# Router products from x1 itself, with the norm moved to weights and logits, and two embedding tiles and the slots' table moved back in TensorE's order

## What is computed

```python
x = x + mix                                    # conv and retention heads, out-projection
x = x + hier_moe(rmsnorm(x, norm2_g), ...)     # 4 groups of 8 experts
ple = rmsnorm(p @ w_ple, ple_norm_g)           # per-layer embedding
x = x + ple * jax.nn.sigmoid(x @ w_ple_gate)

def hier_moe(t, rg_w, rg_b, re_w, re_b, w_gate, w_up, w_down):
    g_prob = softmax(t @ rg_w + rg_b)          # one group
    e_logit = (t @ re_w + re_b)[that group]    # two experts of its eight
    hid = silu(t @ w_gate[e]) * (t @ w_up[e])
    y = (hid * combine) @ w_down[e]
```

## Time and profile before

| what | us |
|---|---|
| median of 3 runs | 692.66 |
| lowest and highest of them | 689.54 and 694.28 |
| the profiled execution, by the clock that timed the runs | 692.57 |
| its span in the trace | 690.8 |
| PE busy in the span | 658.1 |
| DVE, ACT, POOL busy | 575.2, 408.5, 248.6 |

### The profile page before, as it was taken

The page is one execution under the profiler, slowest core; times in us unless marked ns, Lnnn a source line. Parts: engine busy times, 40 slices in busy tenths (PEclk is TensorE's granted clock), DMA queues, the critical chain, the costliest instruction groups (busy, mean ns, idle before and its releaser), DMA issues.

```text
span 690.8 us, 11414 instructions
## 1 busy us (share of the span) xinstructions
PE 658.1 (95%) x3970; PEld 567.8 (82%) x3970; DVE 575.2 (83%) x808; ACT 408.5 (59%) x521; POOL 248.6 (36%) x182
## 2 busy tenths in 40 slices
PE   8999999998999999997999999999999999998996
PEld 5999999998998889846878888888878777766885
DVE  5599999987776474476899999999999999968785
ACT  7331322236262132375699999999999889862322
POOL 1151498979429230004233333333334343310001
PEclk9999999999999999997999999999999999999999
DMA  9651331121039272627489999999999999775211
GB/s 291 201 153 32 129 117 62 62 86 49 1 99 317 77 243 101 234 110 248 173 353 381 374 374 378 367 378 394 394 390 377 379 377 371 292 290 188 77 61 62
DMA packets 49532, 156.10 MB, mean 226 GB/s; under 512 B 6938, under 2 KB 28634, under 8 KB 36427
## 3 DMA queue, kind: packets, MB, share of 16 engines
q1 hardware_dynamic: 35905, 133.98, 51.6%
q10 hardware_dynamic: 9346, 12.13, 5.3%
q0 software_dynamic: 4240, 9.44, 3.8%
HBM read 143.55 MB, written 17.59 MB: 233 GB/s over the span
## 4 chain that ended last, share of the span: by engine, by line
PE 66%; DVE 11%; DMA 9%; issue 6%; ACT 4%; POOL 2%; ACTq 0%; SPq 0%; POOLq 0%; DVEq 0%
PE bank L606 62%; DMA ring<-in_w_expert_up 4%; PE bank L610 4%; DMA ring<-in_w_expert_down 2%; DMA out<-front 2%; ACT catT_parts L2037 1%; DVE front L1777 1%; DVE ring_parts L1445 1%; DVE front L1778 1%; DMA uext<-expert_rows 1%; DVE z L1412 1%; DVE front L1804 1%; POOL z L2403 1%; DMA scratch<-h_rows,sorted_tok 1%; POOL grs L2396 1%
## 5 line engine op out<-in xcount | busy, mean ns | idle before, releaser
L1445 DVE TENSOR_TENSOR ring_parts<-ring,catT_parts 128x2048 fp32r<-128x2048 f32 x64 | 143.6, 2281 | 0.0
L2037 ACT ACTIVATE catT_parts<-ring 128x2048 fp32r<-128x2048 f32 x64 | 122.6, 1916 | 9.1 <-PE bank L606 6.0
L606 PE MATMUL bank<-ring_parts,hT_high 128*128 128x256 f32 (+1 forms) x748 | 113.7, 296 | 0.0
L2449 POOL DMA_INDIRECT expert_rows<-scratch,cur_code x32 | 47.5, 1485 | 181.2 <-issue 126.2
L606 PEld LDWEIGHTS bank<-ring_parts,hT_high 128*128 128x128 f32 x748 | 100.6, 189 | 4.0 <-DVE ring_parts L1315 0.2
L1284 DVE SCALAR_TENSOR_TENSOR bank<-uext,cpar,bank 128x512 f32<-128x512 f32 x116 | 86.0, 741 | 0.0
L1634 DVE TENSOR_TENSOR ring_parts<-ring,down_high 128x2048 fp32r<-128x2048 f32 x30 | 68.8, 2294 | 7.7 <-ACT down_high L2142 6.2
L2296 POOL TENSOR_TENSOR ring_parts<-ring,ring_parts 128x2048 fp32r<-128x2048 f32 x11 | 51.7, 4702 | 58.6 <-ACT ring_parts L1852 58.6
L606 PE MATMUL bank<-ring_parts,catT_parts 128*128 128x256 f32 (+1 forms) x360 | 67.3, 324 | 2.5 <-DVE front_parts L1341 1.3
L606 PE MATMUL bank<-catT_parts,xT_odd 128*128 128x512 f32 x256 | 65.8, 400 | 1.5 <-ACT catT_parts L2037 1.5
L606 PEld LDWEIGHTS bank<-ring_parts,catT_parts 128*128 128x128 f32 x360 | 54.6, 191 | 8.9 <-issue 1.7
(11 more groups left out here) (342 smaller groups left out, 1281.4 us busy)
## 6 DMA issues: line engine op xcount, KB each, us to landing
ring<-in_w_expert_gate SPq DMA_DIRECT2D x32, 1024.0 KB, 5.5
ring<-in_w_expert_up SPq DMA_DIRECT2D x32, 1024.0 KB, 7.5
ring<-in_w_expert_down SPq DMA_DIRECT2D x32, 1024.0 KB, 8.1
ring<-in_w_in SPq DMA_DIRECT2D x12, 1024.0 KB, 7.0
ring<-in_w_out SPq DMA_DIRECT2D x4, 1024.0 KB, 5.0
ring<-in_w_ple_gate SPq DMA_DIRECT2D x4, 1024.0 KB, 7.5
catT<-in_x_prompt SPq DMA_DIRECT2D x4, 512.0 KB, 4.9
z<-in_x_prompt SPq DMA_DIRECT2D x4, 512.0 KB, 5.5
```

What stands on the lines that cost most here:

```text
L606: return nc.tensor.matmul(out, lhsT, rhs, start=start, stop=stop, skip_group_check=True)
L1445: V.tensor_tensor(ring_r[:, 3 * par + m, :], ring[:, 3 * par + m, :], cat_r[:, m * CHUNK:(m + 1) * CHUNK].bitcast(F32), ALU.subtract).then ...
L2037: A.activation(cat_r[:, m * CHUNK:(m + 1) * CHUNK], ring[:, s, :], ACT.Copy).then_inc(S["w_hi"], 1)
L2449: G.indirect_dma_start(moe_d, bass.IndirectOffsetOnAxis(ap=cur_code[0:r, par:par + 1], axis=0), yout[0:r, par, :], None, bounds_check=2 * ...
```

## The change

The router's operand is no longer h2. Its products are made from x1, transposed as it is; the norm's weights g2 are multiplied into `wr` once, and the factor of each row into the logits, where five operations (one for each tile: times `rst2`, plus bias) take the place of two additions. h2 is still formed and stored for the gather. The sample tile's transposes go to one bank (7) and leave it in one copy by DVE. ACT's split of the first expert's weights (`w_high_part(0, 0, ...)`), and DVE's subtraction for the first of the two, move ahead of the sample tile's additions. Behind the ranks PE makes the second half of embedding tile 1 and tile 2, then the sorting table, and tiles 3 and 4 behind it. The slots' table moves behind all transposes, and DVE's one-hot matrices for it behind the first expert's subtractions. The gathered tiles change banks (6 and 7 for even t), and the first one no longer waits for the embedding to be copied out. Each embedding tile is squared in one operation over 1024 columns, not two over 512. The idle products ahead of the first gathered tile become 8.

```diff
         def sorted_banks(t):
-            return pair(2 if t % 2 == 0 else 6)
+            return pair(6 if t % 2 == 0 else 2)
...
         def p_bank(i):
-            return bank[7 if i < TT - 1 else 4]
+            return bank[7 if i < 2 else 5 if i < TT - 1 else 4]
...
-            def h2_T(i):
-                pe.wait_ge(S["h2_done"], i + 1)
+            def x1_T(i):
+                pe.wait_ge(S["x1_sum"], WO.index((15, i)) + 1)
+                if i == TT - 1:
+                    pe.wait_ge(S["pT_sb"], 2)
+                    for k in range(KT):
+                        m = tr(bank[7][:, k * NS:(k + 1) * NS], x1_rows(i)[:, k:D:KT])
+                    m.then_inc(S["h2T_ps"], 1)
+                    return
                 if i:
                     pe.wait_ge(S["h2T_sb"], 2 * i)
                 else:
                     pe.wait_ge(S["rs_upd"], 2 * NH)
-                rows_T(h2[i], i, pair(4), S["h2T_ps"])
+                rows_T(x1_rows(i), i, pair(4), S["h2T_ps"])
...
                 w_out_part(15, i)
                 if i >= 1:
-                    h2_T(i - 1)
+                    x1_T(i - 1)
+            x1_T(4)
             ple_tile(0, (0,))
             router(3)
-            h2_T(4)
             router(4)
             ple_tile(0, (1,))
             p_T((2, 3, 4))
-            ple_tile(1)
+            ple_tile(1, (0,))
...
             m.then_inc(S["rank_done"], 1)
+            ple_tile(1, (1,))
+            pe.wait_ge(S["pT_sb"], TT)
             ple_tile(2)
-            ple_tile(3)
...
             table(laneone, sortone, NT, 2)
+            ple_tile(3)
             ple_tile(4)
...
-            idle_products(14, 4)
-            pe.wait_ge(S["ple_raw"], 2 * TT)
+            idle_products(8, 4)
             pe.wait_ge(S["idx_done"], 1)
             sorted_T(0)
             gate_up_first((0,))
-            table(slotone, blockone, NBLK, 4)
             for t in range(1, 4):
                 sorted_T(t)
             gate_up_first((1,))
             for t in range(4, NT):
                 sorted_T(t)
+            table(slotone, blockone, NBLK, 4)
...
+            dve.wait_ge(S["router_in"], 80)
+            V.tensor_tensor(wr[:, :, :], wr[:, :, :], bc(g2T[:, :], 2, NG + NE), ALU.mult).then_inc(S["zeroed"], 1)
             dve.wait_ge(S["w_hi"], 16)
...
                 if i >= 1:
                     norm2(i - 1)
+                if i == TT - 1:
+                    w_low(0, 0, 0)
                 add_x(14, i)
                 add_x(15, i)
             h2_out_high(TT - 2)
+            sample_h2_out()
             norm2(TT - 1)
-            h2_out_high(TT - 1)
...
-            w_low(0, 0, 0)
             dve.wait_ge(S["logit_done"], TT)
...
-            V.tensor_tensor(logit[:, 0:TT - 1, :], ps[:, 0:TT - 1, :], bc(rbias[:, :], 1, TT - 1), ALU.add).then_inc(S["logit_sb"], 1)
-            V.tensor_tensor(logit[0:NS, TT - 1, :], ps[0:NS, TT - 1, :], rbias[0:NS, :], ALU.add).then_inc(S["logit_sb"], 1)
+            for i in range(TT):
+                r = rows(i)
+                m = V.scalar_tensor_tensor(logit[0:r, i, :], ps[0:r, i, :], rst2[0:r, i:i + 1], rbias[0:r, :], ALU.mult, ALU.add)
+                if i >= TT - 2:
+                    m.then_inc(S["logit_sb"], 1)
...
             x_low_first()
             w_low(0, 0, 1)
+            slot_one_hots()
...
                     h2_store(i - 1)
+                if i == TT - 1:
+                    act.wait_ge(S["wo_done"], WO.index((15, TT - 2)) + 1)
+                    w_high_part(0, 0, 0)
+                    w_high_part(0, 0, 1)
+                    h2_out_low(3)
                 x1_sq(i)
-            h2_out_low(3)
-            w_high_part(0, 0, 0)
             h2_store(4)
-            h2_out_low(4)
-            w_high_part(0, 0, 1)
             ple_out(0)
...
-            for i in range(1, TT):
+            for i in range(1, TT - 1):
                 ple_out(i)
...
-            A.activation(rst4[:, 0:1], epsb[:, :], ACT.Silu)
             x_out_first()
             sorted_half(0)
+            ple_out(TT - 1)
+            A.activation(rst4[:, 0:1], epsb[:, :], ACT.Silu)
             w_high_part(0, 1, 0)
```

55 lines of the change are left out of this document (34 added, 21 removed).

## The result

The changed kernel takes 697.47 us, the median of 9 runs, beside 692.66 for 9 runs of the kernel before. The medians lie 0.7% apart; the ratio worked out from the single runs is 1.0091, 95% interval 1.0059 to 1.0123, so **0.9% slower**, where 691.3 and at most 695.7 were forecast. All ratios leave out runs more than 1.5% above a kernel's fastest: one of the changed kernel's nine (706.1), three of e5's twelve (701.3 to 705.0) and four of the 35 beside e5.

A forecast was written before the change was run, and what follows sets the result against it. PE, holding 66% of the chain, and what it waits for were taken as the bound. 692.57 - 3.0 (earlier first step) + 1.7 (one clock fall) = 691.3 us; eight in ten between 686.6 and 695.7.

The forecast's parts named there:

- Part 1, the first wait (term -1.1): Ahead of the first transposes: PE no longer waits for the norm; 1.1 us taken of the 1.27 us wait.
- Sample tile: Ahead of the sample transposes: PE newly waits some 2.7 us; picks still end net 0.5 us earlier.
- the 0.42 of my bound: DVE's multiplication of the router weights: taken at 0, hidden in a stretched subtraction; 0.42 us if not hidden.
- One fall of three (+1.7): Waits of 2.7, 2.3 and 2.2 us: one brings the clock down, costing 1.7 us; chance 0.40.
- My rival of three falls: Clock falls behind the waits ahead of sample tile, ranks and tile 3: 694.7 us; two or three falls, chance 0.18.
- Part 2: Ranks to first gathered tile: ranks' wait about 2.3 us, table 2.1 us earlier, 3.00 us wait gone, clock held.
- Part 3: First gathered tile to first step: ACT becomes the one waited for; first step at 334.0, 3.0 us earlier.
- ACT's delay: Ahead of gathered tile 3's transposes: PE waits some 2.2 us for ACT's half of tile 1.
- The table load: On ACT's way to tile 3: taken at 1.28 us; the skill's page would bring the first step 1.4 us later.
- The base: Kernel before, 312 to 328: PE ran at 1.2 GHz for 10.2 us and lost 5.1 us of work.

The follow-up runs named there:

- e5: The changed kernel again, no edit, against the kernel before; 697.55 us, ratio 1.0027.
- second traces of both: Traces from repeating the changed kernel (e5) and the kernel before, no edits; 697.55 us and 691.30 us, ratios to before 1.0027 and 0.9994.
- e15: The changed kernel with only the copies of tile 0 moved first on DVE and ACT; 695.07 us, ratio to before 1.0056.
- e3: The changed kernel with ACT's two weight splits and DVE's first subtraction put back behind the sample tile; 693.42 us, ratio to before 1.0034.
- e16: Repeat of e9: changed kernel with splits back, loads late, 18 idle products ahead of the ranks, copies first; 684.71 us, ratio to before 0.9917.
- e2: The changed kernel with both loads of expert 2's weights waiting until the last gather has landed; 694.53 us, ratio to before 1.0017.
- e12: The kernel before with the third gather waiting until the first has landed; 693.63 us, ratio to before 1.0018.
- e4: The kernel before with 39 idle products in place of 14 ahead of the first gathered tile; 692.33 us, ratio to before 1.0019.
- e7: The changed kernel with splits back behind the sample tile, expert 2's loads behind the last gather, 18 idle products ahead of the ranks; 688.16 us, ratio 0.9944.
- e9: e7 with the copies of tile 0 moved first on DVE and ACT; 684.07 us, ratio to before 0.9877.
- e10: e9 with the half of gathered tile 1 sooner on both copying engines; 686.89 us, ratio to before 0.9924.
- e13: The kernel before with the router part, copies first, 36 idle products ahead of the first gathered tile, and expert 2's loads late; 685.17 us, ratio 0.9924.
- e14: The changed kernel, splits left ahead of the sample tile, with copies first, 21 and 18 idle products, loads late; 687.57 us, ratio to before 0.9947.
- e17: The changed kernel with only the second of expert 2's loads waiting for the last gather; 693.87 us, ratio to before 1.0041.
- e8: The kernel before with the router part of the change alone; 689.66 us, ratio to before 0.9982.

## Why the prediction was wrong

The reckoning goes by the second traces of both, unless the first is named.

- **Part 1, the first wait (term -1.1): the step that failed first.** The norm did go from PE's path, but both copies to `hT` still stand behind it. In the first trace the first h2 waits for the store until 264.40, tile 1's additions stand behind it on DVE, tile 1's square behind those on ACT, and ACT's copy behind that: it starts at 267.77. I had this copy end just as PE needs it. Of 1.27 us 0.2 to 0.3 were won, and a fall of 1.7 came behind a wait that I did not have. I named this place only as an example of what would prove me wrong. e15 puts its price at 2.4 us in the medians, which is not clear of noise, and at 2.9 in the traces up to the ranks. How much the copy comes late hangs on when the store lands. In e3, where the order is the same up to there, the first h2 starts 0.2 us ahead of the first transposes (261.24), not 0.8 behind as in e5, and the copy does end as PE needs it.
- **Sample tile.** The wait came as worked out (2.69 for 2.7), with the subtraction and the additions behind split and norm, and no subtraction between logits and sum; the five operations took 0.90 for 0.9. The multiplication of the weights took 1.92 us, not the 0.42 of my bound, but lay beside other work and cost nothing.
- **One fall of three (+1.7): wrong in number.** It fell behind the sample tile and the ranks in every trace in which their waits stayed (2.7 and 2.3 us, in e3 2.6), not at all behind the 1.63 us ahead of tile 3, and also behind the router. Three falls, 5.1 us, and in the first trace a fourth behind the last gather. My rival of three falls gave 694.7.
- **Part 2.** The wait ahead of the ranks was 2.33 for 2.3. From ranks to table I had 5.7 us; it was 7.2, which is 5.5 and the fall. In e16, with no fall, it is 5.5. The wait of 3.00 us went and the clock held there, as forecast.
- **Part 3: the second step that failed.** From the first gathered tile to the first step I had 19.6 us; e2 and e16 take 19.2, the changed kernel 22.3. ACT's delay came (1.63 for 2.2). What I left out is POOL and SP: the embedding tile that moved behind the table holds the third gather, and the gate product that runs at the full clock releases a load 2 to 2.7 us sooner. With one of the two alone the longest landing is 7.7 (e12) or 6.5 us (e4), with both 10.9 (e5), though 9.0 in e3. I had counted the moved tiles as fill for PE's time and not asked who waits for them.
- **The table load.** "ScalarE: Activation LUTs" of the Trainium skill, section "What ACT_TABLE_LOAD costs", would have added 1.4 us. Here in the first trace, the next instruction starts at 328.28, as the load ends (326.99 + 1.28); the row was right to go by. The page gives the drain's length and not its place, but ahead of the load there is no such time either: the instruction before it ends at 326.97.
- **The base.** I took the 10.2 us at 1.2 GHz from one trace. The second has 6.7 us there, and falls at the start and at 164 to 172.

By segments, against the second trace of before, and without the one fall of the forecast, which it put at no one place. To the ranks: -0.5 forecast, +2.9 measured. The 3.4 between them are two falls (3.4) and the first wait (0.8), less the 0.8 by which the kernel before was already late at the last product ahead of the first transposes (263.84 against 263.07), where its fall at 164 to 172 (1.7 us) lay behind it. From ranks to the first gathered tile: -1.1 forecast (12.9 against 13.96), +0.2 measured, a fall of 1.7 less 0.4. From there to the first step: 0.0 forecast (19.6 against 19.64), +2.7 measured, the gathers. The forecast was -1.6 by this base and -3.0 by the first trace, whose fall lasted longer (0.1 and -1.3 with the one fall); measured is +5.8, and 4.8 and 5.3 in the medians.

## What to carry to other kernels

When a change takes an operation off one engine's path, follow what stands behind that operation on the other engines: the wait often moves to their next result. When it makes an engine run sooner or at a fuller clock, list what that engine's progress releases (buffers, loads) and which transfers these will meet. Several short waits can cost more than the one long wait that they replace, since each can bring the clock down.

## What the runs showed of the hardware that was not expected

- The length of a wait did not decide whether the clock falls. Ahead of the first router product, waits of 0.57 (e2) to 1.57 us (e7) were followed by 1.2 GHz, in all six traces that have one; the 1.63 us ahead of gathered tile 3 were not, in any trace that has it, nor were the 0.79 (e4) to 1.97 us (e12) ahead of the first transposes of h2 in the kernel before. Ahead of the first of these waits came eight transposes and then products of 256 columns; ahead of the second came such products and then two tiles of transposes.
- 128 rows gathered by one indirect transfer land in 4.3 to 7.1 us without a load beside them (e2, e7, e9, e10, e13, e14, e16) and in up to 12.3 where a load of 1 MB starts 2 to 3 us behind (e17; 10.3 and more in both traces of the changed kernel; 9.0 in e3; but 6.5 at most in both traces of before, e4 and e8, with such a load).
- Single runs of one kernel spread over 1 to 2% (687.3 to 699.1 for 35 of the kernel before), so a single trace can show falls that the next has not.
